# A pair's gate stands two units behind its weight rows, and VectorE rounds a weight chunk one unit later

## The reference

```python
def _dilated_mixture(q, k, v, rel_bias):
    for gi, (window, dil) in enumerate(DILATED_GROUPS):   # three groups of four heads
        ...
        o, m, den = _dilated_band_attention(...)
        outs.append(o)
        lses.append(m + jnp.log(den))
    wts = jax.nn.softmax(jnp.stack(lses), axis=0)         # across the three groups
    mixed = jnp.concatenate([o * w[..., None] for o, w in zip(outs, wts)], axis=2)

def _attention_sublayer(h, mem_n, w_in, w_out, rel_bias, w_mem_kv):
    q, k, v, q_mem = jnp.split(h @ w_in, ...)
    mixed = _dilated_mixture(q, k, v, rel_bias)
    mem_out = _memory_attention(q_mem, mem_n, w_mem_kv)   # 4 heads, 256 memory rows
    return jnp.concatenate([mixed, mem_out], axis=-1) @ w_out
```

## Time and profile before

| | us |
|---|---|
| median of 3 runs (2723.0 to 2739.25) | 2726.54 |
| the profiled execution | 2727.18 |
| its span | 2725.2 |
| of it, units 0 to 63 of the attention layer: first turn to output projection (1272.0 to 1449.2) | 177 |

### The profile page before, as it was taken

How to read it: one execution, slowest core, us unless ns; L and a number is a source line. 1 busy time by engine, 2 the same in 40 slices (tenths; PEclk the granted TensorE clock), 3 DMA queues, 4 the chain that set the end, 5 groups by cost and what they waited for, 6 DMA issues and landing times.

```text
span 2725.2 us, 32853 instructions
## 1 busy us (share of the span) xinstructions
PE 2518.7 (92%) x12954; PEld 2047.7 (75%) x12954; DVE 1381.8 (51%) x2380; ACT 1068.8 (39%) x1951; POOL 254.0 (9%) x420
## 2 busy tenths in 40 slices
PE   6889899999989989999878999999998998999998
PEld 4677778778556777787657888888876987888887
DVE  3667666554575646562234433325866674533322
ACT  4455442332463445353433322215345452422221
POOL 3143011012000123000000000001001110000000
PEclk9899999999899989999878999999998999999999
DMA  6522365356211412142101333323330000333322
GB/s 242 174 74 69 106 226 176 94 163 197 81 42 54 148 32 62 62 123 59 47 32 49 99 101 93 101 94 102 97 96 9 1 1 16 89 97 97 97 93 77
DMA packets 146225, 250.13 MB, mean 92 GB/s; under 512 B 15455, under 2 KB 65914, under 8 KB 145049
## 3 DMA queue, kind: packets, MB, share of 16 engines
q1 hardware_dynamic: 129008, 198.08, 23.4%
q0 software_dynamic: 14816, 48.31, 5.3%
q10 hardware_dynamic: 2249, 1.65, 0.2%
HBM read 245.84 MB, written 5.30 MB: 92 GB/s over the span
## 4 chain that ended last, share of the span: by engine, by line
PE 77%; DVE 9%; ACT 8%; DMA 4%; issue 3%; POOL 0%; SPq 0%; DVEq 0%; ACTq 0%
PE PS L220 21%; PE PS L221 20%; PE PS L222 20%; PE PS L985 2%; ACT tmp L753 2%; PE PS L1816 1%; PE PS L2378 1%; DVE x L809 1%; DMA hT_a<-in_w_mod 1%; PE PS L2386 1%; PE PS L2391 1%; PE PS L1800 1%; ACT w_hi L205 1%; PE PS L1617 1%; DMA mraw<-in_w_mod 1%
## 5 line engine op out<-in xcount | busy, mean ns | idle before, releaser
L212 DVE TENSOR_TENSOR w_lo<-w_raw,w_hi 128x1024 fp32r<-128x1024 f32 (+1 forms) x344 | 411.8, 1206 | 744.1 <-ACT w_hi L205 743.1
L205 ACT ACTIVATE w_hi<-w_raw 128x1024 fp32r<-128x1024 f32 (+1 forms) x344 | 355.9, 1044 | 978.0 <-DMA w_raw<-in_ffn_w_gate_up 307.8
L220 PE MATMUL PS<-hT_hi,w_hi 128*128 128x512 f32 (+1 forms) x1728 | 663.2, 384 | 21.5 <-DVE hT_lo L821 13.9
L221 PE MATMUL PS<-hT_lo,w_hi 128*128 128x512 f32 (+1 forms) x1728 | 653.6, 378 | 0.0
L222 PE MATMUL PS<-hT_hi,w_lo 128*128 128x512 f32 (+1 forms) x1728 | 653.6, 378 | 0.0
L220 PEld LDWEIGHTS PS<-hT_hi,w_hi 128*128 128x128 f32 x1728 | 331.2, 192 | 88.4 <-issue 22.6
L222 PEld LDWEIGHTS PS<-hT_hi,w_lo 128*128 128x128 f32 x1728 | 330.9, 191 | 59.7
L221 PEld LDWEIGHTS PS<-hT_lo,w_hi 128*128 128x128 f32 x1728 | 331.7, 192 | 56.5 <-issue 0.2
L220 PE MATMUL PS<-w_hi,hT_hi 128*128 128x512 f32 (+1 forms) x704 | 288.0, 409 | 37.2 <-DVE hT_lo L821 10.4
L221 PE MATMUL PS<-w_lo,hT_hi 128*128 128x512 f32 (+1 forms) x704 | 278.1, 395 | 0.0
L222 PE MATMUL PS<-w_hi,hT_lo 128*128 128x512 f32 (+1 forms) x704 | 277.4, 394 | 0.0
(11 more groups left out here) (587 smaller groups left out, 3270.8 us busy)
## 6 DMA issues: line engine op xcount, KB each, us to landing
w_raw<-in_ffn_w_gate_up SPq DMA_DIRECT2D x176, 256.0 KB, 3.1
mraw<-in_w_mod POOLq DMA_DIRECT2D x160, 256.0 KB, 4.1
w_raw<-in_gla_w_in SPq DMA_DIRECT2D x48, 512.0 KB, 4.5
w_raw<-in_ffn_w_down SPq DMA_DIRECT2D x44, 512.0 KB, 3.7
w_raw<-in_fox_w_in SPq DMA_DIRECT2D x32, 512.0 KB, 4.2
w_raw<-in_sgu_w_in SPq DMA_DIRECT2D x24, 512.0 KB, 4.9
w_raw<-in_dn_w_in SPq DMA_DIRECT2D x24, 512.0 KB, 3.5
w_raw<-in_gla_w_out SPq DMA_DIRECT2D x16, 512.0 KB, 4.5
```

What stands on the lines that cost most here:

```text
L205: nc.scalar.activation(w_hi[:, n % NS, :, 0:m], w_raw[:, n % NS, :, 0:m], ACT.Copy).then_inc(w_hidone, 1)
L212: nc.vector.tensor_tensor(w_lo[:, n % NS, :, 0:m], w_raw[:, n % NS, :, 0:m], w_hi[:, n % NS, :, 0:m].bitcast(F32), ALU.subtract).then_inc( ...
L220: nc.tensor.matmul(o, l_hi, r_hi, start=start, stop=False)
L221: nc.tensor.matmul(o, l_hi, r_lo, start=False, stop=False)
```

## The change

Three edits in the attention layer, in which no instruction is added or taken away:

1. `weight_rows(n)` stands at unit NU+6+2n on TensorE (before NU+4+2n), and `gate(n)` at unit NU+8+2n on VectorE (before NU+5+2n). So a gate stands two units behind its weight rows, where it stood one behind, and behind an odd unit's `scale` instead of an even one's. The last two gates are written behind unit 63, ahead of the splits of the memory pairs.
2. `lowest` and `weights` come one unit later on VectorE (NU+3 and NU+4), and their exponential on ScalarE too (NU+3).
3. VectorE rounds a chunk (line 212) at the unit behind that of `FEED_AT`; ScalarE's half stays where it was.

```diff
--- before.py
+++ after.py
@@ -2077,8 +2077,8 @@
                     if u == NU + 1:
                         t_.wait_ge(*fill_taken(7))
                         natural_order()
-                    if u >= NU + 4 and u % 2 == 0 and u < NU + 16:
-                        weight_rows((u - NU - 4) // 2)
+                    if u >= NU + 6 and u % 2 == 0:
+                        weight_rows((u - NU - 6) // 2)
 
                 t_.wait_ge(q.ready, 2)
                 soft.pe([(ps_evac, qk2.ev), (q.toe, 16 * AH)], (ps_evac, v0.ev), between)
@@ -2135,7 +2135,7 @@
                         fill_take(TAKE_AT[u])
                     if u in FEED_AT:
                         act_feed(FEED_AT[u])
-                    if u == NU + 2:
+                    if u == NU + 3:
                         a.wait_ge(q.e1, 1)
                         a.activation(r.Ex, r.Ex, ACT.Exp, scale=-1.0).then_inc(q.e2, 1)
 
@@ -2197,18 +2197,19 @@
                     v.tensor_tensor(hT_lo[:, n, :], hf[:, n % 2, :], hT_hi[:, n, :].bitcast(F32), ALU.subtract).then_inc(q.os, 1)
 
                 def between(u):
-                    if u in FEED_AT:
-                        dve_feed(FEED_AT[u])
+                    if u - 1 in FEED_AT:
+                        dve_feed(FEED_AT[u - 1])
+                    if u == NU + 3:
+                        lowest()
                     if u == NU + 4:
+                        weights()
                         v.wait_ge(w_used, qm.last + 1)
-                    if u == NU + 2:
-                        lowest()
-                    if u == NU + 3:
-                        weights()
-                    if u >= NU + 5 and u % 2 == 1 and u < NU + 16:
-                        gate((u - NU - 5) // 2)
+                    if u >= NU + 8 and u % 2 == 0:
+                        gate((u - NU - 8) // 2)
 
                 soft.dve(between)
+                for n in (4, 5):
+                    gate(n)
                 for n in (6, 7):
                     v.wait_ge(su.po, n + 1)
                     then_dve(v.tensor_copy(hT_hi[:, n, :], r.oT[:, n, :]))
```

## The result

The changed kernel takes 2684.48 us (median of 4 runs, 2682.6 to 2686.53) against 2729.43 us for the kernel before (now 4 runs, 2723.0 to 2739.25): ratio 0.9836, 95% interval 0.9812 to 0.9860. Run again later it took 2683.64 against 2727.67: 0.9825 (0.9796 to 0.9855). The forecast was 2694 with a range of 2679 to 2714, so the sign, the bound of one per cent and the range held, and the gain was larger than forecast: 45.0 us between the medians, 41.6 between the two profiled spans (2725.2 and 2683.6), against 33.

What follows compares the result with a forecast made beforehand. TensorE, busy 92% of the span, was taken to bound the kernel. Terms 14 - 0.5 + 6 + 8.5 + 4 + 1 = 33 us, off the profiled 2727.2, gave 2694 us, range 2679 to 2714.

Steps and rivals of the forecast that it cites:

- pair loop, turn of unit 52 to turn of unit 62: Five attention-layer rounds: each falls from 7.3 to 4.5 us (3.9 to 5.5), gain 14 us (9 to 17).
- tail of the loop: Behind the last `scale`: sixth weight rows and their gate's multiply now stand there, loss 0.5 us (0 to 1).
- turn of 48 to turn of 52: Start of the memory units: 18.0 us falls to 12, gain 6 us (4 to 7).
- chunks of units 1 to 46, with the clock: Units 1 to 46: chunk waits shrink, 8.5 us (4 to 11), and TensorE's clock stays up, 4 us (0 to 8).
- output projection: First products of the output projection: no longer start at the lower clock, gain 1 us, 2.9 at most.
- weight rows 1.90 us (a run of 1.97) to 2.69: TensorE's weight rows in a pair-loop round: 1.90 us at the upper clock, 2.69 at the lower.
- 2.0 us from turn to weight rows: Pair-loop round: first turn, ScalarE's copy, exponential and copy, and hand-overs take about 2.0 us at the upper clock.
- the rival of the wait handed on: Units with chunks: the chunk wait only moves to the next unit; 15.5 us less, 2711 us, chance 18%.
- a chunk fed at an even unit no longer splits a pair of turns: Units with chunks: argument against the wait being only handed on, since TensorE wants score passes in pairs; no size given.
- The 4 us: Slow stretches behind chunk waits, 1316 to 1336 and 1356 to 1367: TensorE's clock stays up, gain 4 us (0 to 8).
- The rival in which the clock stays low: Pair loop: granted clock stays at 0.7, rounds of 5.5 us, no clock term; 21.5 us less, 2706, chance 17%.
- Slower, and nothing: Fills wait for thirteen late chunks, 26 us more, 2753, chance 2%; or gain taken back later, within 5 us, 3%.

Runs made afterwards that it cites:

- filled: Kernel before plus dummy TensorE products that nothing reads, between a memory round's even and odd turn; 2716.05 us against 2727.92, ratio 0.9949.
- gates_only: Changed kernel with the third edit undone, VectorE's chunks back at their old units; 2703.57 us against 2727.15 before, ratio 0.9907.
- gate_one_behind: Changed kernel with each gate one unit behind its weight rows, as before, weight rows still late; 2707.04 us against 2727.15 before, ratio 0.9921.
- filled_scores: Kernel before plus nine dummy TensorE products ahead of the scores of units 21, 35 and 37; 2725.29 us against 2729.13, ratio 0.9983.
- lag_even: Changed kernel with VectorE's chunks late only at even units, odd ones at their old units; 2706.21 us against 2727.92 before, ratio 0.9908.
- chunks_only: Kernel before with the third edit alone, VectorE's half of a chunk one unit later; 2708.56 us against 2727.15, ratio 0.9933.
- lag_two: Changed kernel with VectorE's half of every chunk two units late instead of one; 2685.78 us against 2727.92 before, ratio 0.9832.
- early_start: Changed kernel without the chunks of units 49 and 51, and weights, weight rows and gates one round earlier; 2679.93 us against 2729.13 before, ratio 0.9820.

## Why the prediction was right, and where it was off

Each term of its sum, with what the two profiled executions have at the same places (turn to turn, as the prediction cut them):

| term | forecast | measured |
|---|---|---|
| pair loop, turn of unit 52 to turn of unit 62 | 14 | 17.6 (36.5 to 18.9) |
| tail of the loop | -0.5 | +0.8 (4.8 to 4.0) |
| turn of 48 to turn of 52 | 6 | 7.6 (18.0 to 10.5) |
| chunks of units 1 to 46, with the clock | 8.5 + 4 | 14.3 (118.0 to 103.7) |
| output projection | 1 | 2.9 (30.4 to 27.5) |
| ahead of the first turn | 0 | -2.0 (1272.0 to 1274.0) |
| sum | 33 | 41.1 |

The output projection is taken from its first product to ScalarE's first instruction of the layer behind it (line 732, at 1479.65 before and 1438.57 after). The last row but one is work that the change doesn't move; that mark lies between 1268.5 and 1276.0 in the fourteen traces with no order in it, so it is scatter. What the layer gained stays gained: the gated MLP behind it starts 41.1 us earlier, and the second gated MLP 41.6. (In the prediction's range the low ends add up to 16 us less and not to 15.5, which moves nothing.)

**The pair loop: right mechanism, size too small.** The forecast was 4.5 us a round, between 3.9 at the upper clock and 5.5 at the lower one. Turn to turn it is 3.79 on average, and weight rows to weight rows 3.40, both below the lower bound. The slow end was well placed (5.65 in the round at 0.56), and the fast end was too dear: 3.31 at 1.00. The term that was mis-sized is "weight rows 1.90 us (a run of 1.97) to 2.69": the run of 1.97 us was taken for the price at the upper clock, and it was a mixture of both levels. At a clock of 1.00 the sixteen take 1.53 (filled). The other part of the sum, 2.0 us from turn to weight rows, was 1.71 (1400.72 to 1402.43). ScalarE's copy, exponential and copy are in series as I put them (1401.20 to 1402.34), but each starts about 0.1 us before the one ahead of it ends in the trace, so they take 1.14 us and not 1.26, and the first turn with the hand-overs takes less than I allowed. 1.71 + 1.49 is 3.20, what the round took. gates_only and gate_one_behind show that the gate's place is the cause, at 3.29 and 6.99 us a round.

**The chunks and their clock: right in sum and in split.** 12.5 us forecast, 14.3 measured. From the first turn to the products in natural order 9.1 us of it are idle time (forecast 8.5) and 5.1 busy time (forecast 4), and filled_scores, which fills some of the waits and moves no chunk, took 4.9 us off the same stretch. But one reason given for it carries little. Against the rival of the wait handed on I argued that "a chunk fed at an even unit no longer splits a pair of turns". lag_even has just that; the turns no longer wait there, but it is 2 us of idle time, and the time of the stretch did not fall. The gain needs the late chunks of odd units. Of the 13.0 us for the score pass before, all but the 2.5 at the very start (the 2.7 that I put there is the wait of unit 37) were waits of the scores of units 5, 21, 23, 31, 35 and 37 for the pass three units back, and each of these passes stood right behind the chunk of an odd unit (1, 17, 19, 27, 31 and 33); the rival's own remark, that the largest waits are for scores, pointed there. That odd ones alone would do has not been run.

**The clock, in the loop.** The 4 us were put on A only, and none on the loop beyond the choice of 4.5. filled shows what it was worth from unit 49 on in the kernel before: 7.7 us in C, 2.8 in the output projection (30.4 to 27.6), 1.7 in B and 1.3 in D. The rival in which the clock stays low (2706) is out: the loop's stretch has 0.87, and 1.00 from its second round on. TensorE's stops for ScalarE's copies, which were its ground, don't occur in the loop.

**The rival of the wait handed on (2711) is out in sum, but part of it is there.** Its rule holds: nothing overtakes the chunk, neither in VectorE's queue nor in ScalarE's, where the value products' wait grew from 1.2 us (gates_only) to 6.4. The queue's order is as the Trainium skill has it ("TensorE: Matmul & The Clock Gate", the section on the array's architectural detail, strict FIFOs), and the trace agrees. What the rule does not say is who asks for the results behind the chunk, and when: in chunks_only 18 us of TensorE's waits for turns and scores are gone against before, and 5.4 us came back as waits for copies.

**Slower, and nothing.** TensorE's weight loads waited 0.3 us in all for line 212 between 1318 and 1411 us, and 0.5 us from 1262 on, in the change and in lag_two alike, so a late chunk costs next to nothing here.

**The tail and the first products of the projection** were both taken too dear. 4.7 to 5.6 us were forecast for what stands behind the last `scale`; it took 4.0, again since weight rows at the upper clock take 1.5. And the projection starts at the upper clock (1.00 in its first 4.9 us, 0.50 before): 2.9 us, the upper end of the term. It goes with the tail: 27.5 us in gates_only and gate_one_behind, which have the sixth weight rows there, and 27.6 in early_start, which has them where the kernel before has them but no long idle time behind them (D 4.4), and in filled, whose gaps are filled; 30.4 in chunks_only, whose tail is the old one of 7.5 us. gate_one_behind has it in spite of its slow rounds, so it is the last few microseconds ahead of the projection that go with it; no run changes these alone.

## What to carry to other kernels

Where an engine does helper work of another engine's chain (a gate, a chunk), ask not how much of it there is but which result stands right behind it in the queue and who wants that next; moved by one unit, the same 1.8 us of a gate cost 3.6 us a round or nothing (gate_one_behind and the change). When TensorE and another engine hand work to and fro, a wait of TensorE that is removed can gain twice: its own idle time, and the speed of TensorE's work around it (9.1 us and 5.1 us in units 0 to 48). For the duration of a step at the upper clock take the shortest of its rows in a stretch with a granted clock of 1.00, not the shortest in the stretch that is slow.

## What was not expected of the hardware

- Added work made the kernel faster. Nine products that nothing needs (eighteen instructions in the trace), in the gap of 2.2 us of a round, and sixteen at units 48 and 50, held the granted clock at 1.00 where it had been 0.73, and the kernel took 2716.05 us against 2727.92. Its chain is as before: the odd turn starts 2.84 us behind the even one, as before.
- One instruction group, three durations: the sixteen weight rows take 1.53 us at 1.00, 2.75 in the rounds with idle time, and 1.90 to 2.47 where the clock changes within them. A single row doesn't tell which of these it is, if the granted clock of its stretch isn't read beside it.
- The last three value products and the first weight rows of a round stand in the trace in turns, 0.01 us apart in start (1402.56 and 1402.57), and the sixteen weight rows with three value products among them take 1.49 us, where without them they take 1.46 (filled, 1407.62 to 1409.08). So those three cost almost nothing there. Why they overlap was not tried.
